# A gated delta rule inside a weight-streaming kernel: the block inverse by another recurrence, transposes of whole width with transfers, decay computed on ScalarE

## The reference

```python
g = jnp.cumsum(g.reshape(B, H, N, C), axis=-1)                # log decay, summed in the chunk
decay = jnp.exp(jnp.where(causal, g[..., :, None] - g[..., None, :], -jnp.inf))
k_beta = k * beta
a_mat = jnp.where(strict, jnp.einsum('bhncd,bhnsd->bhncs', k_beta, k) * decay, 0.0)
rhs = jnp.concatenate([v * beta, k_beta * jnp.exp(g)[..., None]], axis=-1)
sol = lax.linalg.triangular_solve(a_mat + jnp.eye(C), rhs, left_side=True, lower=True, unit_diagonal=True)
...
def step(S, xs):                                              # over the chunks
    v_new = u_c - w_c @ S
    o_c = qd_c @ S + qk_c @ v_new
    S = S * gt_c + kt_c.T @ v_new
```

## Time and profile before

| | |
|---|---|
| median of three runs | 1939.63 us |
| span of the profiled execution | 1937.5 us |
| TensorE busy | 1922.7 us (99%), 11140 instructions |
| VectorE busy | 1365.1 us (70%), 1961 |
| ScalarE busy | 935.0 us (48%), 1331 |
| GpSimd busy | 101.1 us (5%), 296 |
| bytes read from and written to HBM | 349.51 and 2.10 MB |

### The profile page before, as it was taken

The page is one execution under the profiler, slowest core; times in us unless marked ns, Lnnn a source line. Parts: engine busy times, 40 slices in busy tenths (PEclk is TensorE's granted clock), DMA queues, the critical chain, the costliest instruction groups (busy, mean ns, idle before and its releaser), DMA issues.

```text
span 1937.5 us, 33061 instructions
## 1 busy us (share of the span) xinstructions
PE 1922.7 (99%) x11140; PEld 1581.1 (82%) x11140; DVE 1365.1 (70%) x1961; ACT 935.0 (48%) x1331; POOL 101.1 (5%) x296
## 2 busy tenths in 40 slices
PE   9999999999999999999999999999999999999997
PEld 7888887888888888888888888888888888888886
DVE  7779889797857777776566766577675466665556
ACT  6555565554455545455544445644443444443442
POOL 0102020010101111111000000000000000000000
PEclk9999999999999999999999999999999999999999
DMA  7444444444554545455655676555555555656555
GB/s 267 154 142 158 149 152 142 154 153 142 186 179 159 188 161 191 159 189 174 190 192 194 216 239 200 181 194 191 191 194 195 194 193 188 196 195 194 194 189 174
DMA packets 98013, 353.19 MB, mean 182 GB/s; under 512 B 10832, under 2 KB 11120, under 8 KB 97776
## 3 DMA queue, kind: packets, MB, share of 16 engines
q1 hardware_dynamic: 97904, 351.65, 55.4%
HBM read 349.51 MB, written 2.10 MB: 181 GB/s over the span
## 4 chain that ended last, share of the span: by engine, by line
PE 95%; DVE 2%; ACT 1%; issue 1%; DMA 1%; SPq 0%; DVEq 0%; ACTq 0%
PE pg L399 88%; PE B L399 5%; DVE gates L1212 1%; DMA raw<-in_weights 1%; PE B L493 0%; ACT whi L800 0%; DVE wlo L1204 0%; PE B L657 0%; ACT hraw L1086 0%; PE B L527 0%; ACT gates L1074 0%; PE B L666 0%; PE B L622 0%; ACT vda L1086 0%; ACT act_a L800 0%
## 5 line engine op out<-in xcount | busy, mean ns | idle before, releaser
L1204 DVE TENSOR_TENSOR wlo<-raw,whi 128x1024 fp32r<-128x1024 f32 (+1 forms) x640 | 779.4, 1221 | 452.1 <-ACT whi L800 433.8
L800 ACT ACTIVATE whi<-raw 128x1024 fp32r<-128x1024 f32 (+1 forms) x640 | 674.4, 1058 | 684.6 <-PE pg L399 673.0
L399 PE MATMUL pg<-whi,act_x 128*128 128x512 f32 x2960 | 950.5, 394 | 1.5 <-ACT whi L800 1.2
L399 PEld LDWEIGHTS pg<-whi,act_x 128*128 128x128 f32 x2960 | 555.3, 188 | 124.3 <-issue 8.9
L399 PE MATMUL pg<-wlo,act_x 128*128 128x512 f32 x1480 | 574.7, 390 | 0.0
L399 PE MATMUL pg<-whi,act_a 128*128 128x512 f32 x1632 | 504.8, 389 | 0.5 <-DVE act_a L1204 0.5
L399 PEld LDWEIGHTS pg<-whi,act_a 128*128 128x128 f32 x1632 | 306.3, 188 | 64.8 <-DVE act_a L1204 1.3
L399 PEld LDWEIGHTS pg<-wlo,act_x 128*128 128x128 f32 x1480 | 278.3, 188 | 53.3
L399 PE MATMUL pg<-wlo,act_a 128*128 128x512 f32 x816 | 317.5, 389 | 0.0
L399 PEld LDWEIGHTS pg<-wlo,act_a 128*128 128x128 f32 x816 | 153.2, 188 | 31.7
L399 PE MATMUL pg<-whi,act_b 128*128 128x512 f32 x512 | 158.4, 389 | 0.0
(11 more groups left out here) (230 smaller groups left out, 1106.5 us busy)
## 6 DMA issues: line engine op xcount, KB each, us to landing
raw<-in_weights SPq DMA_DIRECT2D x646, 512.0 KB, 3.8
gates<-in_ln_in SPq DMA_DIRECT2D x4, 512.0 KB, 5.9
gates<-in_ln_in SPq DMA_DIRECT2D x1, 2048.0 KB, 8.4
out<-gates SPq DMA_DIRECT2D x8, 256.0 KB, 2.8
raw<-in_weights SPq DMA_DIRECT2D x4, 256.0 KB, 4.6
cT<-in_xT SPq DMA_DIRECT2D x2, 512.0 KB, 7.2
qT<-in_xrow SPq DMA_DIRECT2D x2, 512.0 KB, 7.4
kT<-in_xrow SPq DMA_DIRECT2D x2, 512.0 KB, 6.3
```

Source lines behind the costliest of these rows:

```text
L399: return nc.tensor.matmul(o, l, r, start=start, stop=stop)
L800: return nc.scalar.activation(o, i, ACT.Copy, scale=scale)
L1204: return V.tensor_tensor(o, a, b, op)
```

## The change

Four things are changed, all inside the four bodies.

- **Inverse.** The inverse of the 32 x 32 blocks is built from the right: `Pm` holds two halves side by side, `TT` (the inverse so far) and `WT` (the matrix with what has been eliminated). One level is one batch of products of a masked, turned piece `Pc` with both halves, and one subtraction on VectorE. Five batches in slots 17, 19, 20, 21 and 22 (`GROW`): 32, 64, 64, 64 and 32 columns wide. The off-diagonal block follows in slots 23 and 24 (`OFF_P`, `OFF_T`).
- **Decay.** The running sums of the log gates are computed once in the prologue, written to DRAM by ScalarE's own queue as rows, and read back in each body as a broadcast to all partitions (`sums_in`, slot 0). ScalarE computes exp(-relu(gc - row)) in place: eight `Relu` operations of 128 x 128 and one `Exp` of 128 x 1024 (`decays`, slots 4 to 7; in the first body all in slot 13). The four products of slot 12 go.
- **Turning v and the output.** One VectorE operation (two for the output) transposes all 32 x 32 blocks in place into `stage`; a DMA stores `stage` in DRAM, and four DMAs load it back in the other block order: v in slots 22 (`V_BLOCKS`) to 28, the output in slots 11 (`O_BLOCKS`) to 24. These transfers are issued by SyncE between the weight loads.
- **Slots.** The split of the output moves from slots 29 and 30 to 24 and 25; both scalings of v stand in slots 28 and 30 of the same body.

The core of the diff (semaphores and buffers with the same purpose left out):

```diff
+CONV_LINKS, BUILD_LINKS, SCAN_LINKS, DA_LINKS = 12, 19, 7, 25
 OT_SLOTS = (12, 14)
-OT_TURN = {11: 3, 12: 4, 14: 2, 18: 1, 20: 3, 21: 3}
-OT_HI = 29
-V_TURN = {21: 1, 22: 3, 23: 3, 27: 3, 28: 2, 29: 2, 30: 1, 31: 1}
+O_BLOCKS, V_BLOCKS = 11, 22
+O_HI = 24
+V_SCALED = (28, 30)
 TURN = range(1, 7)
 TURN_HI = 8
 GAIN = (11, 13)
 XP = [(0, 2), (2, 4), (4, 8), (8, 12), (12, 16)]
 HALVED = 2
-ROWS = range(2, 6)
+DECAY = range(4, 8)
 WARM = 2
 LATE_LO = 4
-ROUNDS = 5
+GROW = {17: 0, 19: 1, 20: 2, 21: 3, 22: 4}
+GROWN = len(GROW)
+OFF_P, OFF_T = 23, 24
...
+            def blocks_out(scratch, kept):
+                sp.dma_start(scratch.rearrange("a x b c -> (a x) (b c)"), stage[:, :, :, :].rearrange("p b q x -> p (b q x)")
+                             ).then_inc(kept, 16)
+
+            def blocks_in(scratch, dst, full):
+                for b in range(4):
+                    sp.dma_start(dst[b * SB:(b + 1) * SB], scratch[:, :, b].rearrange("a x (q i) -> x a q i", i=SB)
+                                 ).then_inc(full, 16)
+
+            def v_out(j):
+                sp.wait_ge(N["dve_vS"], 1 + j + 1)
+                blocks_out(turn_v, v_kept)
+
+            def v_in(j):
+                sp.wait_ge(v_kept, 16 * (j + 1))
+                blocks_in(turn_v, vtok, v_full)
+
+            def o_out(j):
+                sp.wait_ge(N["dve_oS"], 1 + j)
+                blocks_out(turn_o, o_kept)
+
+            def o_in(j):
+                sp.wait_ge(o_kept, 16 * j)
+                blocks_in(turn_o, oT, o_full)
+
+            for m in range(2, 7):
+                later(m)
+            later(7, range(0, 2))
+            v_out(0)
+            later(7, range(2, 4))
+            v_in(0)
+            with sp.Fori(1, NB) as j:
+                for i in range(3):
+                    later(8 * j + i)
+                later(8 * j + 3, range(0, 3))
+                o_out(j)
+                later(8 * j + 3, range(3, 4))
+                later(8 * j + 4, range(0, 1))
+                o_in(j)
+                later(8 * j + 4, range(1, 4))
+                later(8 * j + 5)
+                later(8 * j + 6)
+                later(8 * j + 7, range(0, 2))
+                v_out(j)
+                later(8 * j + 7, range(2, 4))
+                v_in(j)
+            with sp.Fori(NB * BODY // RING, out_m) as m:
                 later(m)
             sp.wait_ge(N["dve_oT2"], 1 + HEADS)
...
-                    for t in range(TOK):
-                        mm(B[1 + t][:, :], after_r[:, :], flat(g_hi[:, 4 * t:4 * t + 4, :]), True, False)
-                        last = mm(B[1 + t][:, :], after_r[:, :], flat(g_lo[:, 4 * t:4 * t + 4, :]), False, True)
...
+                if s in GROW:
+                    k = GROW[s]
+                    f0, f1 = SB if k == 0 else 0, SB if k == GROWN - 1 else CH
+                    pe.wait_ge(N["dve_x"], 1 + GROWN * j + k + 1)
+                    waits_end()
+                    for i in range(8):
+                        for q in range(4):
+                            a = sub(q)
+                            last = mm(B8[1][a, i, f0:f1], Pc[a, i, :], Pm[a, i, f0:f1])
+                    last.then_inc(N["pe_x"], 1)
+                if s == OFF_P:
+                    pe.wait_ge(N["dve_t"], 1 + 2 * j + 1)
+                    waits_end()
+                    for i in range(8):
+                        for q in (0, 2):
+                            last = mm(C8[2][sub(q + 1), i, :], AT[sub(q), i, sub(q + 1)], Tc[sub(q), i, :])
+                    last.then_inc(N["pe_p"], 1)
+                if s == OFF_T:
+                    pe.wait_ge(N["dve_p"], 1 + j + 1)
+                    waits_end()
+                    for i in range(8):
+                        for q in (0, 2):
+                            b = sub(q + 1)
+                            last = mm(C8[1][sub(q), i, :], Pc[b, i, :], TT[b, i, :])
+                    last.then_inc(N["pe_t"], 1)
                 if s == 27:
...
+            def decays(j, part, parts):
+
+                if part == 0:
+                    act.wait_ge(sums_full, 16 * (j + 1))
+                    act.wait_ge(N["dve_g"], 1 + j + 1)
+                for i in range(8 // parts * part, 8 // parts * (part + 1)):
+                    last = nc.scalar.activation(decm[:, i, :], decm[:, i, :], ACT.Relu, bias=gcur[:, i:i + 1], scale=-1.0)
+                if part == parts - 1:
+                    last.then_inc(N["act_past"], 1)
+                    act.wait_ge(N["act_past"], 1 + j + 1)
+                    nc.scalar.activation(decm[:, :, :], decm[:, :, :], ACT.Exp, scale=-1.0).then_inc(N["act_decay"], 1)
+
...
+                    if isinstance(j, int):
+                        decays(j, 0, 1)
                 if s == 25:
...
+                    ch(tt(Tc[:, :, :], WT, rep(masks[:, 0, :], 8), ALU.mult))
+                    V.transpose(flat(Pc[:, :, :]), flat(Tc[:, :, :])).then_inc(N["dve_x"], 1)
+                    ch(tt(TT, rep(masks[:, 6, :], 8), Tc[:, :, :], ALU.subtract))
+                if s in GROW:
+                    k = GROW[s]
+                    dve.wait_ge(N["pe_x"], 1 + GROWN * j + k + 1)
+                    if k == GROWN - 1:
+                        ch(tt(TT, TT, B8[1][:, :, 0:SB], ALU.subtract))
+                        V.transpose(Tc[:, :, :], TT).then_inc(N["dve_t"], 1)
+                    else:
+                        if k == 0:
+                            ch(tt(WT, WT, B8[1][:, :, SB:CH], ALU.subtract))
                         else:
-                            V.tensor_copy(Pc[:, :, :], C8[1]).then_inc(N["dve_p"], 1)
-                    else:
-                        dve.wait_ge(N["pe_t"], 1 + ROUNDS * j + r + 1)
-                        if r < ROUNDS - 1:
-                            ch(tt(TTc[:, :, :], TTc[:, :, :], C8[2], ALU.subtract))
-                            V.transpose(flat(Tc[:, :, :]), flat(TTc[:, :, :])).then_inc(N["dve_t"], 1)
...
+                if s == V_BLOCKS:
+                    dve.wait_ge(N["act_silu"], 1 + 3 * j + 2)
+                    if not isinstance(j, int):
+                        dve.wait_ge(o_kept, 16 * j)
+                    V.transpose(stage[:, :, :, :].rearrange("p b q x -> p q b x"),
+                                cT[:, 1].rearrange("p h (q b x) -> p (h q) b x", q=TOK, x=SB)).then_inc(N["dve_vS"], 1)
...
+                if not alone and s == O_BLOCKS:
+                    dve.wait_ge(N["dve_oh"], 1 + 2 * j + 2)
+                    dve.wait_ge(v_kept, 16 * (j + 1))
+                    for t in range(TOK):
+                        last = V.transpose(stage[:, :, :, :].rearrange("p b (h t) x -> p h t b x", t=TOK)[:, :, t],
+                                           od[:, t].rearrange("p h (b x) -> p h b x", x=SB))
+                    last.then_inc(N["dve_oS"], 1)
+                if not alone and s == O_HI + 1:
```

More of the change, by code:

```diff
@@ L135, in build @@
         zs = tmp("zs", [P, 2, NG])
-        g_hi, g_lo = (dn.enter_context(nc.sbuf_tensor(n, [P, 8, P], F32R)) for n in ("g_hi", "g_lo"))
-        g_r = dn.enter_context(nc.sbuf_tensor("g_r", [P, TOK * HEADS], F32R))
+        stage = tmp("stage", [P, 4, 8, SB])
+        oT = tmp("oT", [P, 4, 8, SB])
         dn.close()
@@ L220, in build @@
         warm = flat(TTf[:, :, :])
+        centre, sums = (flat(QKT[:, :, :])[:, i * P:(i + 1) * P] for i in range(2))
+        vtok = flat(kT[:, :, :]).rearrange("p (a q x) -> p a q x", a=4, x=SB)
+        turn_v, turn_o = (nc.dram_tensor(n, (4, SB, 4, 8 * SB), F32).ap() for n in ("turn_v", "turn_o"))
+        sums_out = nc.dram_tensor("sums_out", (NB, 8 * P), F32).ap()
         def xt(a, b):
@@ L260, in build @@
         const_full = sem("const_full")
+        sums_kept = sem("sums_kept")
+        sums_full = sem("sums_full")
+        v_kept, v_full, o_kept, o_full = (sem(n) for n in ("v_kept", "v_full", "o_kept", "o_full"))
         ln_full = sem("ln_full")
@@ L472, in prologue @@
                     mm(B[3][:, 0:32], c("same"), g_all[:, :])
-                    mm(B[3][:, 32:64], c("after"), g_all[:, :]).then_inc(N["pe_sc0"], 1)
+                    mm(B[3][:, 32:64], c("after"), g_all[:, :])
+                    mm(B[3][:, 64:96], centre, g_all[:, :]).then_inc(N["pe_sc0"], 1)
+                if s == 9:
+                    pe.wait_ge(N["act_gc"], 1)
+                    nc.tensor.transpose(B[3][0:SB, P:2 * P], pz[:, 1, :], ident).then_inc(N["pe_gT"], 1)
                 if s == 12:
@@ L969, in dn_scan @@
                     copy(hi(act_a, HB * j, HB, t * P, (t + 1) * P), B4[2 + t]).then_inc(N["act_oT"], 1)
-                if not alone and s == OT_HI:
-                    act.wait_ge(N["dve_od"], 1 + j + 1)
-                    copy(hi(act_a, HB * j, HB), qT[:, :, :]).then_inc(N["act_oT"], 2)
+                if not alone and s == O_HI:
+                    act.wait_ge(o_full, 64 * (j + 1))
+                    copy(by_block(hi(act_a, HB * j, HB)), by_source(oT)).then_inc(N["act_oT"], 2)
             def body(n, evac_fn, mixes=()):
```

(22 more changed lines are left out.)

202 lines of the change are left out of this document (63 added, 139 removed).

## The result

| | before | after |
|---|---|---|
| median of the runs, us | 1939.74 (4 runs) | 1961.36 (4 runs) |
| profiled execution, span, us | 1937.5 | 1959.0 |
| mean granted clock in it | 0.998 | 0.993 |

A forecast was written before the change was run, and what follows sets the result against it. TensorE was taken to bound the kernel, VectorE close behind; -9.0 + 3 x (4.1 + 0.7 + 1.4) + 4.7 = +14.3 us, on 1937.5 plus 2.1, gave 1953.9 us, range 1938 to 1966.

The forecast's parts named there:

- rival (a): Slot 14: the clock falls in TensorE's new wait, slowing products by 3 us three times, term 3 goes; 1961 us, chance 0.17.
- term 2: Slots 11 to 14: loads of tiles 15 and 16 queue behind the output's store; +4.1 us in each of three bodies.
- term 3: Slots 17 to 20: VectorE is late for TensorE's slot 20; +0.7 us in each of three bodies.
- Term 1: All four bodies: TensorE loses decay products and three inverse batches, 2.34 us a body; -9.0 us in total.
- the row that did bear on it: End of the earlier run: after the last product the clock stayed 0.99 for 3.0 us, then 0.50.
- Term 4: Slots 24 to 28: the output's moved split makes Pm late for slot 28; +1.4 us in each of three bodies.
- Term 5: First body: decay behind the squares in slot 13 brings waits of 2.4 and 2.3 us, slots 17 and 20; +4.7 us.
- Rival (b): The output's four loads delay tiles 17 and 18, VectorE late at slot 17; 1962 us, chance 0.09.
- Rival (d): Inverse: seven batches cost as ten because waits for VectorE replace them; 1960 us, chance 0.05.
- Rival (c): Not slower: new waits total under term 1's 9.0 us; 1934 us, chance 0.19 with its neighbourhood, 0.14 faster.

The follow-up runs named there:

- experiment 10: Changed kernel, store behind tile 18's load, output halves in slots 29 and 30, first-body decay differences in slot 12, inverse's third and later batches a slot later: 1930.69 us.
- Experiment 5: Changed kernel, SyncE's wait kept ahead of tile 15's load, only the output's store and four loads moved behind the loads of tiles 18 and 20: 1955.45 us.
- experiment 1: Changed kernel with the output's store and its wait behind tile 18's load, the four loads back behind tile 20's: 1939.39 us.
- experiment 4: Changed kernel with the output's store and its wait between the loads of tiles 15 and 16: 1950.98 us.
- experiment 9: experiment 8's kernel with the strips of transposes moved out of slots 18 to 22: 1952.52 us.
- experiment 3: Changed kernel with both edits, the store behind tile 18's load and the output's halves in slots 29 and 30: 1935.98 us.
- experiment 8: experiment 3's kernel plus first-body decay differences in slot 12, with values and output turned by 16 strips each instead of transfers: 1939.96 us.
- Experiment 2: Changed kernel with the output's halves in slots 29 and 30, as before the change, instead of 24 and 25: 1958.65 us.
- experiment 7: Kernel before with the new inverse alone, its old decay and strips of transposes kept: 1939.72 us.

## Why the prediction was right, and where it was not

The sign, the place and the mechanism were as forecast, and the time lay in the range. But the case that came true is rival (a), 1961 us at a chance of 0.17, and not the one put first, 1954 at 0.50. The 7.4 us between are four misses: the slow products behind the wait, left out of the sum (+6.9), term 2 (+3.0), term 3 (-2.1, by which luck made the error smaller), and -0.4 in terms 1, 4 and 5 together. Term by term:

- **Term 1, TensorE's work: right.** Forecast 2.34 us less a body. Where nothing waits (experiment 10), TensorE is busy 110.52, 110.57 and 110.86 us in the bodies 2 to 4, from slot 28 to slot 28, instead of 113.08, 113.35 and 113.06: 2.6, 2.8 and 2.2 less. The assumed wide batch is right too: 1.27 us were taken, and the chain of after, third body, shows 1.03 and 2.96 for the tile behind it, 1.26 above a bare tile of 2.73:

```profile
314.64 1.03 PE B L462 x64
315.67 2.96 PE pg L462 x12
```

- **Term 2, the weight stream behind the store: right in kind, too small.** Forecast 4.1 us (its own times, 285.8 less 281.83, give 4.0), measured 4.65, 4.80 and 5.82, 5.1 on average, at the high end of its bounds (5.2). The step that was short is the landing of tile 16: 6.1 us from the store's issue were forecast (276.4 to 282.5), and ScalarE began the tile 6.9 us after it (284.97 to 291.88). Experiment 5, with the store and the four loads behind tiles 18 and 20, leaves 3.8 us of a body's wait, and experiment 1 shows the term as a whole to come from the queue's order.
- **The clock: the step that failed.** The sum had nothing for it. The k·k products take 2.0 us more (3.78 against 1.78) and the tiles behind them 0.3 (5.73 against 2 x 2.73). Of the 2.0 some 0.3 go with any wait, whatever the clock (2.05 in experiment 4), and 1.7 with the clock. That the clock is at 1.00 in all four bodies of before was no evidence, since nowhere in it does TensorE stand still for long before the end; the row that did bear on it, pointed the right way, and was given too small a chance. The Trainium skill, "TensorE: Matmul & The Clock Gate" ("HAM oscillation — how this bites in real kernels"), describes a kernel whose products start slow again after every wait for a transfer. The trace of after agrees, with three of three waits of 4.65 us or more, and experiment 5's with three of 3.8 to 3.9. For shorter waits the runs don't settle it: 2.22 us lowered the clock in experiment 4, 2.28 and 3.11 did not; of experiment 9's three waits of 2.52 us at slot 28 only the first did.
- **Term 3, slot 20 in the later bodies: wrong in this kernel, but real.** Forecast +0.7, measured 0. TensorE's long wait at slot 14 let VectorE catch up, as rival (a) said. With that wait gone, slot 20 is late again: 0.2 us with the transfers (experiment 3), 1.4 without (experiment 8).
- **Term 4, slot 28: right.** Forecast 1.4 (its own line of working ends at 1.5), measured 1.5. Experiment 2 shows the moved halves to be its cause.
- **Term 5, the first body: right in its sum.** Forecast 2.4 and 2.3, measured 2.3 at slot 17, but 1.4 at slot 20; 0.3 at slot 28 and 0.5 at a convolution, which were not forecast, bring it to 4.5 against 4.7.

For the third body: -2.8 + 4.8 + 2.0 + 0.3 + 1.5 = +5.8, against 6.05 measured. Rival (b) did not come true: behind the four loads ScalarE waited 0.3 to 0.4 us for tile 17, and TensorE nowhere at slot 17 of the later bodies. Rival (d) did not come true for the change as it was made, since TensorE's wait at slot 14 hid it, but it is exactly what happens to the new inverse alone (experiment 7). Rival (c)'s point of decision holds: with the waits below the saving the kernel is faster, experiment 10.

What stays open: why the clock fell at some waits of 2.2, 2.3 and 2.5 us and not at others of 2.3, 2.5 and 3.1. And experiment 10 still has the first body's waits of 0.2 to 0.8 us, which were not worked on further.

## What to carry to other kernels

An engine's queue of transfers is in order: a store that waits for a late result holds back every load behind it. Put it behind the loads that must not be late and count from there; here moving the store and the loads that follow it was worth 22 us of 1961. A saving of the bounding engine's work is paid out in full only where the engine behind it keeps up. So look at the rows of both, and shift the link that is late by a slot before giving up the change. And add to every wait of several us in front of TensorE what the clock costs after it.

## What the runs showed of the hardware

- Each time that the clock fell in the bodies, it was down for either 3.4 or 6.8 us, in every kernel here. The first body's wait of 2.3 us at slot 17 is the clearest case of how alike waits differ. In the changed kernel and in experiments 2 and 4 it left the clock at 1.00; in experiments 1, 3 and 5 the same wait of the same code lowered it for 3.4 us. In experiment 1 that cost 0.2 us for the small products behind it and 1.4 us of busy time in the whole first body, but TensorE's later waits there shrank by nearly as much (slot 20: 0.6 us instead of 1.4), and slot 28 came only 0.1 us later (110.07 against 109.98). Changed kernel, then experiment 1:

```profile
68.06 0.74 PE L462 MATMUL B<-Pm,Pc 32*32 32x32 f32 x64 [2.29 <-DVE Pc L1456]
```

```profile
68.12 0.93 PE L462 MATMUL B<-Pm,Pc 32*32 32x32 f32 x64 [2.30 <-DVE Pc L1456]
```

- Widening a batch of 64 small instructions (32 x 32 tiles) from 32 to 64 moving columns made the batch 1.10 us long instead of 0.75, so half again for twice the work.
